# The down layer of a hybrid transformer step on one core: Strassen's products on pairs of token tiles

## The chip, the core and the metric

The kernel runs on one core of a Trainium2 chip. A core has TensorE (PE, 128 x 128 matmuls into PSUM), VectorE (DVE), ScalarE (ACT), GpSimd (POOL) and SyncE (SP, which issues most DMAs); all work from their own queues, in order, and wait for each other by semaphores. The metric is the device time of one execution in microseconds (us). The kernel before was timed three times: 1558.73, 1561.91 and 1562.32, median 1561.91.

## The reference

One inference step of one layer: a mixer (retention and sparse attention), then a feed-forward block. Only the second matmul of that block is changed:

```python
h = x + rms_norm(mix, g_post_mix)
f = rms_norm(h, g_pre_ffn) @ w_up
f = jnp.square(jax.nn.relu(f)) @ w_down
y = h + rms_norm(f, g_post_ffn)
```

There are 1024 prompt tokens and 128 new ones, so 9 tiles of 128 tokens; `w_up` is 1024 x 4096 and `w_down` 4096 x 1024, all in float32. `f` has 4096 features.

## The kernel before

Each float32 operand x of a matmul is split in two: hi = x rounded to the engine's format (a copy by ACT) and lo = x - hi (a subtraction by DVE or POOL). A product then takes three matmuls, hi x hi, hi x lo and lo x hi (`three_products`, L389 to L391).

The up layer goes in 16 steps of 256 features. It already uses Strassen's algorithm on its own blocks: per step seven products over the 8 prompt tiles (12 matmuls of 512 columns each) and the ninth tile directly ("odd"). Four blocks of the step's features (2 x 128 features by 2 x 512 tokens) are formed from PSUM banks and kept copies, passed through relu and square, and collected in `f_out`. The three blocks c11, c12 and c22 are formed by an addition and squared by DVE (`squared`, L2538), the fourth by ACT (`corner`). ACT issues the store of a step to the scratch `f_d` (L2428). POOL makes lo of the up layer's weights (L2145); DVE adds the up weights' combinations (L2128).

The down layer has the same 16 steps of 256 features. For step n SP loads 256 rows of `w_down` (`weights_in`, 1 MB) and the step's rows of f for all nine tiles (`rows_in`, 1.2 MB). ACT rounds the weights (`weights_hi`, L2760, 128 x 2048), POOL subtracts (L2804), ACT rounds the rows of three tiles at a time (`rows_hi`, L2769, 128 x 768), DVE subtracts (`rows_lo`, L2774). For each tile PE makes two column halves of 512, each of 2 feature blocks x 3 matmuls, into one of four double PSUM banks `dn`; DVE adds the 128 x 1024 result to the accumulator `acc` in SBUF (L2832; L2830 copies in the first step). PE waits for `added` of the tile four before. The order of every engine is written by hand: the functions `scalar`, `gpsimd`, `vector`, `tensor` of `up_programs` are followed by those of `down_programs`. Two functions, `room.down_hi` and `room.down_lo`, prepare the first weights and rows inside the last step of the up layer.

In the last step ACT sums the squares of each finished tile (L2789), POOL makes the reciprocal root (L2808, L2811), DVE multiplies by it and the gain (L2838), and DVE or POOL adds the residual h (L2816, L2844), which SP has loaded; SP stores the tile.

Of the kernel before, what the change touches and what calls it, by code (L numbers as in the profile page):

```python
# [23 lines left out]
P = 128  # L24
D = 1024
# [109 lines left out]
def hybrid_layer_kernel(nc, a, o):  # L135
# [18 lines left out]
    f_d = nc.dram_tensor("f_scratch", [STEPS, P, FC, TOK], F32, kind="Internal").ap()  # L154
# [1858 lines left out]
FIRST = [0, 1, 6, 7]  # L2013
FIRST_PRODUCTS = 9
# [22 lines left out]
class Room:  # L2037
# [361 lines left out]

def up_programs(nc, wide, paired, w_up, sem, ident, room, f_d):  # L2400
# [37 lines left out]
    def room_free(eng, n):  # L2438
# [492 lines left out]
```

## Time and profile before

| what | value |
|---|---|
| median of 3 runs | 1561.91 us (1558.73 to 1562.32) |
| profiled execution | 1557.19 us |
| its span | 1555.3 us |
| mean granted clock of TensorE | 0.987 |
| PE busy | 1495.5 us, 96% |
| DVE, ACT, POOL busy | 857.7, 708.1, 575.2 us |

The span runs from the first to the last instruction of the profiled execution; the time holds 1.9 us around it. A busy PE is one with a matmul in flight: matmuls overlap, each is shown 0.39 us long where the next starts 0.23 later. The granted clock is a share of 2.4 GHz; 0.50 is 1.2 GHz.

### The profile page before, as it was taken

Reading aid. Unit: us, or ns where it says so; the run is one execution under the profiler, and the core shown is the slowest. Engines: PE = TensorE matmul, PEld = TensorE weight load, DVE = VectorE, ACT = ScalarE, POOL = GpSimd, SP = SyncE. Lnnn points to the kernel's source line nnn. Section 1 sums busy time; section 2 is a strip of 40 time slices with the busy share of each in tenths; the row PEclk is TensorE's granted clock in tenths of the full one; section 3 lists DMA queues with packets and bytes.
Section 4 is the critical chain, followed back from the end, with each engine's and each line's share of the span. In section 5 each row is a group of like instructions: output and inputs, shape, how many; then the busy total and the mean of one; then the engine's idle time right before and its main releaser. Section 6 shows DMA issues by size and latency. Waiting matters only on the chain.

```text
span 1555.3 us, 22691 instructions
## 1 busy us (share of the span) xinstructions
PE 1495.5 (96%) x7956; PEld 1251.0 (80%) x7956; DVE 857.7 (55%) x1673; ACT 708.1 (46%) x1515; POOL 575.2 (37%) x509
## 2 busy tenths in 40 slices
PE   7998999999998999999999999999999999999994
PEld 6985787877777788978878888888888888888883
DVE  5278677777875555323574333342355555555557
ACT  5467577767676876624353333433322211121112
POOL 2311366656532541023455545554522122121215
PEclk9999999999998999999999999999999999999997
DMA  7310312121136542043312332233252231312216
GB/s 223 92 28 13 106 38 53 49 53 45 41 76 133 140 111 61 8 154 115 117 49 108 115 112 71 106 115 113 103 191 75 98 115 59 115 61 112 105 65 202
DMA packets 115304, 145.68 MB, mean 94 GB/s; under 512 B 46040, under 2 KB 93560, under 8 KB 110968
## 3 DMA queue, kind: packets, MB, share of 16 engines
q1 hardware_dynamic: 111120, 124.36, 25.7%
q10 hardware_dynamic: 4072, 19.88, 3.2%
q8 instruction: 64, 1.05, 0.3%
q14 instruction: 48, 0.39, 0.1%
HBM read 105.96 MB, written 38.25 MB: 93 GB/s over the span
## 4 chain that ended last, share of the span: by engine, by line
PE 63%; DVE 2%; ACT 2%; issue 2%; POOL 2%; SPq 1%; DMA 0%; POOLq 0%; ACTq 0%; DVEq 0%
PE wide L389 10%; PE wide L390 10%; PE wide L391 10%; PE paired L389 8%; PE paired L390 8%; PE paired L391 8%; PE paired L1984 4%; PE wide L1957 2%; PE paired L1968 2%; POOL acc L2816 0%; POOL ob_h L2322 0%; PE paired L2248 0%; DVE qT L1837 0%; SPq L1625 0%; DVE ob_mT_lo L2336 0%
## 5 line engine op out<-in xcount | busy, mean ns | idle before, releaser
L2804 POOL TENSOR_TENSOR aT_lo<-raw_u,aT_hi 128x2048 fp32r<-128x2048 f32 x16 | 73.8, 4613 | 294.7 <-ACT aT_hi L2760 294.7
L2769 ACT ACTIVATE xb_hi<-f_raw 128x768 fp32r<-128x768 f32 x48 | 40.7, 848 | 300.6 <-PE wide L391 153.7
L2145 POOL TENSOR_TENSOR wu_lo<-raw_u,wu_hi 128x512 fp32r<-128x512 f32 x64 | 86.5, 1371 | 164.5 <-ACT wu_hi L2140 164.5
L389 PE MATMUL paired<-w_hi,aT_hi 128*128 128x512 f32 x320 | 132.6, 414 | 1.4 <-PEq L424 1.4
L391 PE MATMUL paired<-w_hi,aT_lo 128*128 128x512 f32 x320 | 127.1, 397 | 0.0
L2832 DVE TENSOR_TENSOR acc<-wide,acc 128x1024 f32<-128x1024 f32 x68 | 83.3, 1224 | 79.0 <-PE wide L391 79.0
L390 PE MATMUL paired<-w_lo,aT_hi 128*128 128x512 f32 x320 | 126.6, 396 | 0.0
L2832 DVE TENSOR_TENSOR acc<-paired,acc 128x1024 f32<-128x1024 f32 x67 | 82.0, 1224 | 76.6 <-PE paired L391 76.6
L389 PE MATMUL wide<-aT_hi,xb_hi 128*128 128x512 f32 x288 | 112.2, 389 | 0.2 <-DVE acc L2832 0.2
L389 PE MATMUL paired<-aT_hi,xb_hi 128*128 128x512 f32 x288 | 112.1, 389 | 0.0
L391 PE MATMUL wide<-aT_hi,xb_lo 128*128 128x512 f32 x288 | 112.0, 389 | 0.0
L390 PE MATMUL paired<-aT_lo,xb_hi 128*128 128x512 f32 x288 | 112.0, 389 | 0.0
L390 PE MATMUL wide<-aT_lo,xb_hi 128*128 128x512 f32 x288 | 112.0, 389 | 0.0
L391 PE MATMUL paired<-aT_hi,xb_lo 128*128 128x512 f32 x288 | 112.0, 389 | 0.0
L1070 ACT ACTIVATE spare<-scores,sl_key 128x768 bf16<-128x768 f32 (+2 forms) x96 | 100.3, 1045 | 11.2 <-DVE sl_key L1176 3.8
L374 POOL TENSOR_TENSOR w_lo<-stage,w_hi 128x512 fp32r<-128x512 f32 (+1 forms) x50 | 64.4, 1304 | 100.1 <-ACT w_hi L369 100.1
L2145 POOL TENSOR_TENSOR wu_lo<-w_sum,wu_hi 128x512 fp32r<-128x512 f32 x60 | 90.1, 1532 | 0.0
L1199 DVE TENSOR_SCALAR_CACHE_REDUCE spare<-scores,sl_key 128x384 bf16<-128x384 f32 (+3 forms) x128 | 86.9, 679 | 4.6
L2564 DVE TENSOR_TENSOR f_out<-wide,stage 128x512 f32<-128x512 f32 x15 | 10.4, 691 | 126.6 <-PE wide L391 126.6
L389 PEld LDWEIGHTS paired<-w_hi,aT_hi 128*128 128x128 f32 x320 | 60.6, 189 | 18.2 <-issue 5.0
L1984 PE MATMUL paired<-vt,pT 128*128 128x64 f32 x576 | 72.9, 272 | 1.0 <-ACT pT L1741 0.6
L1984 PEld LDWEIGHTS paired<-vt,pT 128*128 128x128 f32 x576 | 70.0, 193 | 2.5 <-ACT pT L1741 1.2
(332 smaller groups left out, 4126.6 us busy)
## 6 DMA issues: line engine op xcount, KB each, us to landing
f_scratch<-f_out ACTq DMA_DIRECT2D x16, 1152.0 KB, 4.2
f_raw<-f_scratch SPq DMA_DIRECT2D x16, 1152.0 KB, 5.1
raw_u<-in_w_up SPq DMA_DIRECT2D x16, 1024.0 KB, 5.3
raw_u<-in_w_down SPq DMA_DIRECT2D x16, 1024.0 KB, 7.3
stage<-in_w_in SPq DMA_DIRECT2D x32, 256.0 KB, 3.3
stage<-mix_scratch SPq DMA_DIRECT2D x9, 512.0 KB, 4.1
h_scratch<-ob_h SPq DMA_DIRECT2D x9, 512.0 KB, 2.9
out<-acc SPq DMA_DIRECT2D x9, 512.0 KB, 5.0
```

The costliest lines, as they stand in the source:

```text
L374: self.nc.gpsimd.tensor_tensor(lo, raw, hi.bitcast(F32), ALU.subtract).then_inc(self.lo_done, 1)
L389: nc.tensor.matmul(out, lhs[0], rhs[0], start=first, stop=False, skip_group_check=onto)
L390: nc.tensor.matmul(out, lhs[0], rhs[1], start=False, stop=False, skip_group_check=onto)
L391: return nc.tensor.matmul(out, lhs[1], rhs[0], start=False, stop=last, skip_group_check=onto)
L1070: nc.scalar.activation(act_junk[:, 0:P * (t + 1)], score[t][:], ACT.Sign, scale=-1.0, bias=limit, accum_out=c_sum[:, n:n + 1]).then_inc(sl ...
L1199: nc.vector.tensor_scalar(dve_junk[:, 0:cells.shape[1]], cells, limit, None, ALU.is_ge, ALU.add, accum_out=c_sum[:, n:n + 1]).then_inc(sl_ ...
L1957: mm = nc.tensor.matmul(qk[u % 2][:, c0:c0 + w], qT[:, (t + 1) % 2, KV * m + g], kT[k][:, g, c0:c0 + w], start=(k == 0), stop=(k == 1))
L1984: mm = nc.tensor.matmul(po[:, h * HD:(h + 1) * HD], pT[:, n % 3, k * P:(k + 1) * P], vt[:, k0 + k, 64 * g:64 * g + 64], start=(k0 + k == 0 ...
L2145: self.nc.gpsimd.tensor_tensor(self.room.wu[1][:, s], self.source(i), self.room.wu[0][:, s].bitcast(F32), ALU.subtract).then_inc(self.lo_d ...
L2769: nc.scalar.activation(fT[0][:, q % 2], raw_f[n % 2][:, :, g * GT:(g + 1) * GT], ACT.Copy).then_inc(f_hi, 1)
L2804: nc.gpsimd.tensor_tensor(wd[1][n % 2], raw_d, wd[0][n % 2].bitcast(F32), ALU.subtract).then_inc(d_lo, 1)
L2832: nc.vector.tensor_tensor(acc[:, t], dn[d % 4][:], acc[:, t], ALU.add).then_inc(added, 1)
```

## The change

Two steps of 256 features are taken together as a double step d. In it the matrix of f^T has blocks by step (n = 0, 1: which half of the contraction inside a product) and by feature block (first or second 128 of a step), and the weights are B11, B12 (first feature blocks, left and right 512 columns), B21, B22 (second). Token tile k is paired with tile k+4. For such a pair Strassen's (Winograd's) form needs seven products in place of eight:

- of the rows: A11, S1, S3, A12, S2, S4, A22, where the S are sums and differences of the four blocks. They don't depend on the weights, so the up layer forms them, and stores seven blocks per pair of tiles (`COMB = 7`), 3968 columns a step where it stored 2304. DVE does it with three `add`s of 128 x 512 after c22 (`sums`), one later (`last_sum`), and one of 128 x 128 for the odd tile (`odd_sum`).
- of the weights: B11, T1, B21, T3, T2, B22, T4. DVE makes the four T per double step (`weight_sum`, 128 x 1024); ACT and POOL split all seven (128 x 1024 each).
- each product is 2 (steps) x 3 matmuls of 512 columns into one PSUM bank. Three of them go on a bank that holds an earlier product (T2 on the bank of B11, B22 on that of T1, T4 on that of T3); so each waits until DVE has added that earlier product.
- DVE adds every one of the seven banks to one of the accumulators c11, c12, c21, c22 or to a common part `acc_u`, which is added to the other three quarters once, in the last double step (`spread`).
- the ninth tile (the odd one) is computed with four products of the plain weights and of B22 with T3.

The rows come per tile pair (`rows_hi`/`rows_lo` of 128 x 1792), and the store of a step is issued after the third kept copy of the next step, not after the odd tile's.

```diff
+COMB = 7
+A11C, S1C, S3C, A12C, S2C, S4C, A22C = range(COMB)
+PAIR = COMB * P
+ODD = 4 * PAIR
+ROW = ODD + 3 * P
...
+        def sums(n):
+            if n == 0:
+                dve.wait_ge(f_act, 1)
+            dve.wait_ge(marked, mark["c22", n])
+            add(block(n, S1C), a21, block(n, A22C), ALU.add)
+            add(block(n, S3C), a21, block(n, A11C), ALU.subtract)
+            dve.wait_ge(marked, mark["S1", n])
+            add(block(n, S2C), block(n, S1C), block(n, A11C), ALU.subtract)
...
     def store(act, n):
-        act.wait_ge(squared_done, 3 * (n + 1))
+        act.wait_ge(marked, max(mark["S4", n], mark["odd", n]))
...
+SPLIT_ORDER = ("B11", "B21", "T1", "T3", "T2", "B22", "T4")
+PRODUCTS = (("B11", A11C, "a"), ("T1", S1C, "b"), ("B21", A12C, "c"), ("T3", S3C, "d"), ("T2", S2C, "a"), ("B22", S4C, "b"),
+            ("T4", A22C, "d"))
...
+    units = [(d, k) for d in range(LAST_STEP) for k in (0, 1, ODD_TILE, 2, 3)] + [(LAST_STEP, k) for k in (0, 1, 2, 3, ODD_TILE)]
...
+    def weights_in(sp, d):
+        for n in (1, 0):
+            if d >= 1:
+                sp.wait_ge(d_lo, COMB * d)
...
+            sp.dma_start(raw_d[:, n], down_rows(w_down, (2 * d + n) * FB)).then_inc(d_in, 16)
...
+        weights_hi(act, 0, "B22")
+        weights_hi(act, 0, "T4")
+        for u, (d, k) in enumerate(units):
+            if u + 1 < len(units):
+                rows_hi(act, u + 1)
+            if d < LAST_STEP:
+                for w in {1: ("B11", "B21"), ODD_TILE: ("T1", "T3"), 3: ("T2", "B22", "T4")}.get(k, ()):
+                    weights_hi(act, d + 1, w)
+            elif k != ODD_TILE:
+                sums(2 * k)
+                sums(2 * k + 1)
...
+        weight_sum(dve, 0, "T4")
+        for u, (d, k) in enumerate(units):
+            if u + 1 < len(units):
+                rows_lo(dve, u + 1)
+            if d == LAST_STEP and 1 <= k < ODD_TILE:
+                normalize(2 * k - 2)
+                normalize(2 * k - 1)
+            if k != ODD_TILE:
+                add_pair(u, d, k)
+                if d == LAST_STEP:
+                    spread(u, k)
+            else:
+                add_odd(u, d, 0)
+                add_odd(u, d, 1)
+            if d < LAST_STEP:
+                for w in {1: ("T1", "T3"), ODD_TILE: ("T2",), 2: ("T4",)}.get(k, ()):
+                    weight_sum(dve, d + 1, w)
...
+                if name in opened:
+                    pe.wait_ge(added, sums_before[u] + {"a": 1, "b": 2, "d": 4}[name])
```

**ACT at the turn from up to down.** Before (xb_hi<-f_raw are rows, aT_hi<-raw_u weights of down, L2467 to L2516 belong to up's last step):

```order
L2760 ACTIVATE aT_hi<-raw_u_2239 128x2048 [waits ml_product,ix_relued]
L2769 ACTIVATE xb_hi_2234<-f_raw0_2254 128x768 [waits ml_product,ix_iw_out]
L2467 ACTIVATE stage<-wide0 128x256 [waits ix_p_turned,ml_product]
L2469 ACTIVATE stage<-stage 128x256 [waits ix_p_kept_lo]
L2460 ACTIVATE f_out1_2253<-paired1 128x512 [waits ix_added,ml_product]
L2462 ACTIVATE f_out1_2253<-f_out1_2253 128x512 [waits ix_s_scored]
L2516 ACTIVATE f_out1_2253<-wide0 128x2x128 [waits ix_p_turned]
L2428 DMA f_scratch<-f_out1_2253 128x2304 [waits ix_past_in1,ix_p_new,ix_s_weighted]
L2769 ACTIVATE xb_hi_2234<-f_raw0_2254 128x768 [waits ml_product,ix_iw_out]
```

And now (raw_d are plain weights, t_sum the T, w_all the rows of a pair):

```order
L2889 ACTIVATE xb_hi_2234<-t_sum0_2260 128x1024 [waits ml_product,ml_u_sum]
L2504 ACTIVATE stage<-wide0 128x256 [waits ix_p_turned,ml_product]
L2506 ACTIVATE stage<-stage 128x256 [waits ix_p_kept_lo]
L2889 ACTIVATE xb_hi_2234<-t_sum1_2261 128x1024 [waits ml_product,ml_u_sum]
L2889 ACTIVATE aT_hi<-t_sum2_2262 128x1024 [waits ml_product,ml_u_sum]
L2497 ACTIVATE f_out1_2253<-paired1 128x4x128 [waits ix_added,ml_product]
L2499 ACTIVATE f_out1_2253<-f_out1_2253 128x4x128 [waits ix_s_scored]
L2559 ACTIVATE f_out1_2253<-wide0 128x256 [waits ix_p_turned]
L2465 DMA f_scratch<-f_out1_2253 128x3968 [waits ix_past_in1,ix_p_new,ix_s_weighted]
L2889 ACTIVATE aT_hi<-raw_d_2257 128x1024 [waits ml_product,ix_relued]
L2889 ACTIVATE aT_hi<-t_sum0_2260 128x1024 [waits ml_product,ml_u_sum]
L2907 ACTIVATE wu_hi_2241<-w_all_2258 128x1792 [waits ml_product,ix_q_kept]
```

The rows of pair 1 (last line) now stand behind the store of the last step and two weights.

**DVE in a steady double step.** Before, one lo of 768 (xb_lo) and three adds alternate:

```order
L2774 TENSOR_TENSOR xb_lo_2235<-f_raw0_2254,xb_hi_2234 128x768 [waits ix_q_turned]
L2832 TENSOR_TENSOR acc_2257<-paired0,acc_2257 128x1024 [waits ix_q_hi]
L2832 TENSOR_TENSOR acc_2257<-wide1,acc_2257 128x1024 [waits ix_q_hi]
L2832 TENSOR_TENSOR acc_2257<-wide0,acc_2257 128x1024 [waits ix_q_hi]
L2774 TENSOR_TENSOR xb_lo_2235<-f_raw0_2254,xb_hi_2234 128x768 [waits ix_q_turned]
```

Now, from the last add of pair 1 (L3008) to the first of pair 2:

```order
L3008 TENSOR_TENSOR acc5_2268<-wide0,acc5_2268 128x512 [waits ix_z_kept_lo,ix_q_hi]
L2927 TENSOR_TENSOR t_sum0_2260<-raw_d_2257 128x1024 [waits ix_wT_in,ix_relued]
L2927 TENSOR_TENSOR t_sum1_2261<-raw_d_2257 128x1024 [waits ix_wT_in,ix_relued]
L2913 TENSOR_TENSOR aT_lo<-w_all_2258,aT_hi 128x1792 [waits ix_q_turned]
L3008 TENSOR_TENSOR stage<-wide1,stage 128x512 [waits ix_z_kept_lo,ix_q_hi]
L3008 TENSOR_TENSOR stage<-paired0,stage 128x512 [waits ix_z_kept_lo,ix_q_hi]
L2927 TENSOR_TENSOR t_sum2_2262<-raw_d_2257,t_sum0_2260 128x1024 [waits ml_u_sum,ix_wT_in,ix_relued]
L2913 TENSOR_TENSOR wu_lo_2242<-w_all_2258,wu_hi_2241 128x1792 [waits ix_q_turned]
L3008 TENSOR_TENSOR acc2_2265<-paired0,acc2_2265 128x512 [waits ix_z_kept_lo,ix_q_hi]
```

Three weight sums and two lo of 1792 stand where one lo of 768 stood; the lo of pair 3 (L2913, second) comes ahead of pair 2's first add.

**ACT in the last double step.** Before, the squares (L2789) follow each other, with one piece of rows between:

```order
L2769 ACTIVATE xb_hi<-f_raw_2255 128x768 [waits ix_q_hi,ix_q_kept] x2
L2789 ACTIVATE dump,fn_st<-acc 128x1024 [waits ix_z_kept_lo]
L2789 ACTIVATE dump,fn_st<-acc 128x1024 [waits n_lo,ix_z_kept_lo] x2
L2769 ACTIVATE xb_hi<-f_raw_2255 128x768 [waits ix_q_hi,ix_q_kept]
L2789 ACTIVATE dump,fn_st<-acc 128x1024 [waits n_lo,ix_z_kept_lo] x6
```

Now the squares (L2955) of two tiles stand ahead of the rows (L2907) of each following pair:

```order
L2907 ACTIVATE wu_hi<-w_all 128x1792 [waits ix_q_hi,ix_q_kept]
L2955 ACTIVATE fn_dump,fn_st<-acc_2263 128x1024 [waits ix_z_kept_lo]
L2955 ACTIVATE fn_dump,fn_st<-acc_2267 128x1024 [waits n_lo,ix_z_kept_lo]
L2907 ACTIVATE aT_hi<-w_all 128x1792 [waits ix_q_hi,ix_iw_out]
L2955 ACTIVATE fn_dump,fn_st<-acc_2264 128x1024 [waits n_lo,ix_z_kept_lo]
L2955 ACTIVATE fn_dump,fn_st<-acc_2268 128x1024 [waits n_lo,ix_z_kept_lo]
L2907 ACTIVATE wu_hi<-w_all 128x1792 [waits ix_q_hi,ix_q_kept]
```

The first L2907 is pair 1's rows, the second pair 2's; before pair 2's rows ACT waits for pair 0's finished tiles.

## Rows read from the trace of the kernel before

**Rows 1.** The page, first part: busy time, share of the span, instructions.

```profile
PE 1495.5 (96%) x7956; PEld 1251.0 (80%) x7956; DVE 857.7 (55%) x1673; ACT 708.1 (46%) x1515; POOL 575.2 (37%) x509
```

**Rows 2.** Windows: stretch, length, busy of each engine (count), clock, DMA share, GB/s.

```profile
1200.00:1500.00 300.00, 300.00 (x1325) 248.43 (x1324) 167.38 (x148) 53.09 (x49) 55.35 (x12) 1.00 0.26 96
```

**Rows 3.** Groups by line and shape, 1200 to 1500: busy, mean ns, idle before.

```profile
L389 PE MATMUL wide<-aT_hi,xb_hi 128*128 128x512 f32 x224 | 87.1, 389 | 0.0
...
L2832 DVE TENSOR_TENSOR acc<-wide,acc 128x1024 f32<-128x1024 f32 x56 | 68.6, 1225 | 67.3 <-PE wide L391 67.3
...
L2804 POOL TENSOR_TENSOR aT_lo<-raw_u,aT_hi 128x2048 fp32r<-128x2048 f32 x12 | 55.4, 4613 | 238.4 <-ACT aT_hi L2760 238.4
...
L2774 DVE TENSOR_TENSOR xb_lo<-f_raw,xb_hi 128x768 fp32r<-128x768 f32 x37 | 35.1, 950 | 0.0
L2769 ACT ACTIVATE xb_hi<-f_raw 128x768 fp32r<-128x768 f32 x37 | 31.4, 849 | 247.0 <-PE paired L391 126.3 <-PE wide L391 120.8
L2760 ACT ACTIVATE aT_hi<-raw_u 128x2048 fp32r<-128x2048 f32 x12 | 22.8, 1903 | 0.0
```

**Rows 4.** Timeline of the turn from up to down: start, duration, [idle before].

```profile
1133.95 4.61 POOL L2804 TENSOR_TENSOR aT_lo<-raw_u,aT_hi 128x2048 fp32r<-128x2048 f32 x1 [9.22 <-ACT aT_hi L2760]
...
1134.19 0.69 DVE L2571 TENSOR_TENSOR f_out<-paired,stage 128x512 f32<-128x512 f32 x1 [6.99 <-PE paired L391]
...
1134.91 4.20 DVE L2538 SCALAR_TENSOR_TENSOR f_out<-f_out 128x512 f32<-128x512 f32 x1
...
1139.76 0.19 PEld L389 LDWEIGHTS paired<-aT_hi,wu_hi 128*128 128x128 f32 x1 [0.23 <-DVE f_out L2576]
...
1142.78 0.48 PE L389 MATMUL paired<-aT_hi,xb_hi 128*128 128x512 f32 x1
```

**Rows 5.** Timelines of DVE and of POOL in up; POOL's L2145, min/median/max ns.

```profile
843.66 0.69 DVE L2128 TENSOR_TENSOR w_sum<-w_sum,raw_u 128x512 f32<-128x512 f32 x1
...
846.00 1.77 DVE L2128 TENSOR_TENSOR w_sum<-raw_u 128x512 f32<-128x512 f32 x1
...
845.49 1.74 POOL L2145 TENSOR_TENSOR wu_lo<-raw_u,wu_hi 128x512 fp32r<-128x512 f32 x1
...
L2145 POOL TENSOR_TENSOR wu_lo<-w_sum,wu_hi x60: 1282/1730/1753, 802.4 to 1118.0; 128x512 fp32r<-128x512 f32 x60
```

**Rows 6.** DMA issues from 1177 to 1186: packets, KB each, us to landing.

```profile
DMA packets 416, 2.23 MB, mean 248 GB/s; under 512 B 32, under 2 KB 32, under 8 KB 288
...
raw_u<-in_w_down SPq DMA_DIRECT2D x1, 1024.0 KB, 7.1
```

**Rows 7.** Windows at two granted clocks, and PE's timeline at two gaps.

```profile
490.30:500.60 10.30, 9.49 (x42) 8.27 (x42) 6.17 (x23) 5.60 (x21) 0.00 (x0) 0.50 0.32 64
...
792.40:800.00 7.60, 5.32 (x28) 4.49 (x28) 5.28 (x5) 6.93 (x11) 1.74 (x3) 1.00 0.61 192
...
1538.30:1555.00 16.70, 0.00 (x0) 0.00 (x0) 13.89 (x12) 3.46 (x6) 6.49 (x7) 0.50 0.86 288
...
490.95 0.48 PE L1957 MATMUL wide<-kT_hi,qT 128*128 128x128 f32 x1 [1.91 <-DVE kT_lo L1837]
...
794.78 1.09 PE L2248 MATMUL paired<-ident,ob_x 128*128 128x128 f32 x8 [2.28 <-DVE ob_x L2351]
```

**Rows 8.** Timeline of the end, by engine.

```profile
1529.49 0.19 PEld L389 LDWEIGHTS wide<-aT_hi,xb_hi 128*128 128x128 f32 x1 [0.64 <-DVE acc L2832]
...
1534.85 0.39 PE L391 MATMUL paired<-aT_hi,xb_lo 128*128 128x512 f32 x1
...
1529.47 1.06 ACT L2789 ACTIVATE dump<-acc 128x1024 f32<-128x1024 f32 x1 [7.89 <-DVE acc L2832]
1530.44 0.18 ACT L2789 ACTIVATION_READ_ACCUMULATOR dump<-acc 128x1 f32 x1
...
1550.98 1.28 DVE L2854 SCALAR_TENSOR_TENSOR acc<-acc,fn_st,raw_u 128x1024 f32<-128x1024 f32 x1
...
1530.53 2.42 POOL L2816 TENSOR_TENSOR acc<-acc,raw_u 128x1024 f32<-128x1024 f32 x1
```

More of the change, by code:

```diff
@@ L2523, in scalar @@
         keep_odd(STEPS - 1)
+        store(act, STEPS - 1)
     def gpsimd(pool):
@@ new lines, in gpsimd, with add, add_pair, spread @@
+        for k in range(3):
+            rescale(2 * k)
+            rescale(2 * k + 1)
+            residual(2 * k)
+            residual(2 * k + 1)
+        for i in range(6, TILES):
+            rescale(i)
+        residual(6)
+    def vector(dve):
+        def add(cells, bank, u, i, opens):
+            dve.wait_ge(dn_done, products[u] + i + 1)
+            if opens:
+                nc.vector.tensor_copy(cells, bank).then_inc(added, 1)
+            else:
+                dve.wait_ge(added, sums_before[u] + max(0, i - 1) if i < 4 else sums_before[u])
+                nc.vector.tensor_tensor(cells, bank, cells, ALU.add).then_inc(added, 1)
+        def add_pair(u, d, k):
+            b, zero = banks[k % 2], d == 0
+            if zero and k in (1, 2):
+                dve.wait_ge(f_stored[k - 1], 16 * (STEPS // 2))
+            c11, c12, c21, c22 = acc[k][:, left], acc[k][:, right], acc[k + 4][:, left], acc[k + 4][:, right]
+            add(c11, b["a"], u, 0, zero)
+            add(c22, b["b"], u, 1, zero)
+            add(c11, b["c"], u, 2, False)
+            add(c22, b["d"], u, 3, False)
+            add(acc_u[k], b["a"], u, 4, zero)
+            add(c12, b["b"], u, 5, zero)
+            add(c21, b["d"], u, 6, zero)
+        def spread(u, k):
+            for i, cells in enumerate((acc[k][:, right], acc[k + 4][:, left], acc[k + 4][:, right])):
+                dve.wait_ge(added, sums_before[u] + COMB)
+                nc.vector.tensor_tensor(cells, cells, acc_u[k], ALU.add).then_inc(added, 1)
+        def add_odd(u, d, m):
+            add(acc[PT][:, (left, right)[m]], banks[0]["dc"[m]], u, m, d == 0)
+        def normalize(i):
+            t = finals[i]
+            if i == 0:
@@ L2857, in vector @@
-        for q in range(Q - 1):
-            rows_lo(dve, q + 1)
-            if q == Q - 2:
-                for t in range(3):
-                    normalize(t)
-            for j in range(3):
-                add(3 * q + j)
-        last = 3 * (Q - 1)
-        normalize(3)
-        residual(3)
-        normalize(4)
-        add(last)
-        residual(4)
-        normalize(5)
-        add(last + 1)
-        residual(5)
-        weigh(6)
-        add(last + 2)
-        scaled_residual(6)
-        weigh(7)
```

494 lines of the change are left out of this document (312 added, 182 removed).

## The prediction

> **What bounds the kernel now.** I read the page's busy shares first, then the stages by windows, then the groups of the down layer, then order of time at its two ends. TensorE (PE) is busy for 96% of the span [rows 1], and 300 us inside the down layer hold 1325 matmuls with no gap at the full granted clock [rows 2]: one matmul of 512 columns every 300/1325 = 0.2265 us. There VectorE (DVE) is busy 167 us of 300, ScalarE (ACT) 53, GpSimd (POOL) 55, and DVE's adds wait for PE, not the reverse [rows 2, 3]. So a matmul removed from this layer is worth its 0.2265 us as long as PE is never kept waiting by the three others, which hold the operands' second halves (ACT rounds to "hi", DVE or POOL subtracts to get "lo"). The layer starts at 1142.78 [rows 4], its last matmul starts at 1534.85, and the span ends 20.1 us after that matmul's end, at 1555.3 [rows 8]. The profiled execution took 1557.19, 4.7 below the median of the runs shown (1561.91).
>
> **Part 1, matmuls.** Before: 9 tiles x 2 column halves x 2 features x 3 = 108 per step, 216 per pair of steps. After: 4 tile pairs x 7 products x 6, plus 24 for the odd tile = 192. Eight double steps: 192 fewer, x 0.2265 = **-43.5 us**, if nothing stalls. A product is 6 matmuls, 1.36 us; a tile pair 9.51; the odd tile 5.44.
>
> **Part 2, what the others must deliver.** Durations of new shapes by line through neighbours of the same kind. DVE with 512, 768 and 1024 elements: 0.69, 0.95, 1.22 [rows 3, 5], so 1.04 per 1000; an lo of 1792 is 2.0 (bounds 0.95 and 2.2, the same slope at 2048), a weight sum of 1024 is 1.2. ACT: 0.85 for 768, 1.90 for 2048 [rows 3], so 1.68 for 1792, 1.06 for 1024. POOL: 1.28 for 512, 4.61 for 2048 [rows 3, 5], so 2.4 for 1024. Two consecutive operations of one engine overlap by 0.1. A product's result reaches another engine 0.2 after PE turned to the next (a matmul shows 0.39 for 0.2265 of spacing). In a double step of 43.5 us this makes some 34 us on DVE, 15 on ACT and 17 on POOL. All fit; only collisions can cost.
>
> The collision: a DVE operation with both inputs in SBUF waits while POOL runs. POOL ran 1133.95 to 1138.56, and DVE's squaring, begun at 1134.91, took 4.20 instead of 0.69 [rows 4]. When both queue, they alternate: POOL's at 845.49 takes 1.74 after DVE's, DVE's at 846.00 takes 1.77, not 0.69 [rows 5]; of 60 POOL splits the median is 1.73 against 1.28 at least [rows 5]. DVE's adds from PSUM stay at 1.22 [rows 3]. The Trainium skill, "SBUF — State Buffer", Who interferes with whom, says the same: a VectorE instruction with two SBUF inputs and a GpSimd one that reads SBUF exclude each other for a whole instruction. By that rule, the trace agrees, the change pays with DVE's time for what it adds to POOL: seven splits of 1024 in a double step (16.8 us) instead of two of 2048 (9.2). The order of the changed kernel puts DVE's next-but-one lo *ahead* of the adds of the current pair, and product 5 of each pair (T2, on the bank of product 1) waits for the first add. So the pair stalls when first add ends later than 5.44 us after its start.
>
> **Part 3, steady double steps.** Time t from the start of pair 0. POOL splits T2 (-1.4 to 1.0), B22 (to 3.4) and T4; ACT, after T4's hi, rounds the rows of pair 1 until 2.9; DVE's lo gets in at 3.4, ends 5.3, first add 5.9: PE stalls 0.5. T4's lo ends at 7.5 and releases 2 MB of weights. Before, 2.2 MB in two issues landed 7.1 us after the second [rows 6]; so they are there at 14.3, and B11 and B21 are split by 20.3, just before DVE is done with pair 1 (20.4). DVE: sums T1, T3, lo of pair 2 until 24.7; PE needs it at 25.0: no stall. Then POOL's T1 lo (to 26.9), DVE's sum T2 (to 28.0), POOL's T3 lo (waiting longer, to 30.3), DVE's lo of pair 3 (to 32.2), first add of pair 2 to 32.9; product 5 was due at 30.45: **stall 2.4**. Pair 3 has no stall. Sum over seven double steps with a successor, or predecessor: 7 x 2.4 + 7 x 0.5 = **+20.2** (bounds: 7 x 0.2 = 1.4 without exclusion; 7 x 5, twice 2.4 and more, if the weights land 3 us later).
>
> **Part 4, the turn from up to down**, in the trace's own times. Step 15 of up: c12 is added at 1134.19. DVE's squaring waits for POOL's B11 (to 1136.1), then POOL's B21 goes first (1136.7 to 1139.0), DVE: lo of pair 0 to 1140.9, sum T1 to 1142.0, and only then c22, which up's last product waits for: it starts at 1142.65 instead of 1139.76 [rows 4]. POOL T1 to 1145.6, DVE sum T3 and T2 to 1147.8, S1C, then alternately POOL T3, S3C, POOL T2, S2C, S4C, the odd sum at 1155.2. ACT stands at the store of step 15 until then, and behind the store are B22, T4 and the rows of pair 1 (0.5+1.06+1.0+1.7: 1159.3). POOL's T4 holds DVE until 1161.4, lo of pair 1 to 1163.3, first add 1164.0. PE did four products of pair 0 from 1145.5 and waits from 1152 to 1164.1 for the fifth, due at 1142.78+5.44 = 1148.2: **+15.9** (bounds: 4.2, the same chain with no exclusion; 20, if each lo meets one more POOL operation).
>
> **Part 5, the last double step.** ACT's queue is rows(k+1), squares of two tiles, rows(k+2); the squares wait for the last add and a spread add of pair k. From the end E of a pair: add to E+0.9, spread to 1.6, squares of two tiles (1.06+0.18 each [rows 8]; the second waits for the third spread) to 4.15, rows hi to 5.85, lo to 7.9, two normalizations of 1.28 (as the last line of DVE's kind in [rows 8]) to 10.3, first add to 10.9. Product 5 is due at E+5.44: **5.5** twice; before the odd tile the rows are 768 wide, **3.6**. Sum +14.6 (bounds 11, 18). The 0.6 stall in the last step of before [rows 8] goes. After the last matmul come one add, ACT's square, and DVE normalize, normalize, weigh, residual, scaled residual with POOL's 2.42 [rows 8] in between: 9.2, and 3.0 for the store as before (1550.98+1.28 to 1555.3): 12.2 against 20.1, **-7.9**.
>
> **Other edits.** Up's steps: DVE gets four sums of 0.69, alternating with POOL, up to 1122; its next due work is at 1125.9. The store leaves 2 us later with 2.0 instead of 1.2 MB and is due 16 us after. Nothing: PE waits nowhere there today, and DVE has those gaps. If the cover fails, c22 late by 1 us costs 15.
>
> **Part 6, the clock.** PE was granted 1.2 GHz from 490.3 for 10.3 us around a gap of 1.91 us, though it worked densely again; a gap of 2.28 at 792.5 left it at 2.4 [rows 7]. After PE's end it fell, too [rows 7]. The 12 us wait of part 4 will lower it, and each us at 1.2 GHz after resuming costs half of it: between 0 and 5, I take 3. The three waits of part 5: four products at half speed cost up to 4.1 a pair, I take 2 each: +6 (0 to 17, the odd tile included). Waits of 2.4: 0 (up to 1.7 each). The skill, "TensorE: Matmul & The Clock Gate", Why this matters for your kernels, asks that gaps between bursts stay short, else the array falls back; by it, parts 4 and 5 pay and part 3 does not.
>
> **Sum.** -43.5 +20.2 +15.9 +14.6 -0.6 -7.9 = -1.3 at the full clock, +9 for the clock: +7.7, 1557.19 -> 1564.9 for a profiled execution, and with the same 4.7 between it and the median: **1569**.
>
> **Rivals.** (A) The waits overlap as summed, but the clock stays at 2.4 GHz: 1561.9-1.3 = 1560.6. For: 2.28 us without a fall. Against: 12 us is far more. (B) The exclusion hardly bites, because the orders fall otherwise: bounds of parts 3 and 4, 18.8+11.7 less: 1569-30-3 = 1536. For: DVE has 9 us free per double step; against: rows 5. (C) Half: the 2.4 of part 3 vanish, for its order hangs on 0.1 us here and there: 1552. (D) Slower than all: PE falls to 1.2 GHz in the stalls of pair 2 and in most of the last double step: 7 x 1.7 + 11 + 2 more: 1594. It decides as soon as waits of 2.4 lower the clock.
>
> **How the numbers follow.** Forecast 45%, A 19%, C 14%, B 10%, D 12%. 0.3% is 4.7 us, about what a measurement tells. Faster: B, C and a little of A, 0.27; same: most of A and the forecast's lower edge, 0.19; slower: the rest, 0.54. Cases of both signs count, so the forecast's own range is 1560 to 1580; the range for all is 1543 to 1590.
>
> **What would show it.** Right: matmuls 192 fewer; a PE gap near 12 us between T3 and T2 of the first pair, released by DVE's first add; gaps of 2 to 3 before product 5 of each pair 2 (bank of paired0, right half), of 0.5 in pair 0; 5.5, 5.5, 3.6 in the last double step; DVE's 1792-wide lo at 2.0 alone and 4 beside POOL; granted clock at 0.5 after the first gap. Wrong: no gaps in the steady double steps (B, C), lo durations all at 2.0, or PE waiting for weights (then the landing of 2 MB was mis-sized), or waits inside the up layer.

## The result and the profile after

Before 1560.74 us median (4 runs, 1558.73 to 1562.32), after **1582.62 us** (4 runs, 1581.24 to 1585.71): ratio 1.0144, 95% interval 1.0123 to 1.0164. The kernel is 22 us (1.4%) slower; 7.7 had been forecast. The direction, the range for all cases (1543 to 1590) and most of the terms held; the size did not, and the median lies above the forecast's own range (1560 to 1580). The profiled execution took 1582.76 with a span of 1581.0, so it took 25.6 longer than that of before (1557.19).

The page's first part after [rows 1], of span 1581.0 us, busy time, share and instructions:

```profile
PE 1475.8 (93%) x7764; PEld 1224.8 (77%) x7764; DVE 1018.4 (64%) x1881; ACT 752.9 (48%) x1547; POOL 678.9 (43%) x553
```

PE has less to do, and DVE 160 us more than before. The same 300 us stretch of the down layer as in [rows 2] (stretch, length, busy of PE, PEld, DVE, ACT, POOL with counts, clock, DMA share, GB/s), and its groups of POOL and DVE [rows 3] (mean ns behind the comma):

```profile
1200.00:1500.00 300.00, 279.38 (x1184) 225.25 (x1183) 229.16 (x241) 88.91 (x73) 127.13 (x42) 0.98 0.36 125
```

```profile
L3008 DVE TENSOR_TENSOR acc<-wide,acc 128x512 f32<-128x512 f32 x95 | 65.1, 685 | 42.6 <-PE wide L391 42.6
L2975 POOL TENSOR_TENSOR aT_lo<-t_sum,aT_hi 128x1024 fp32r<-128x1024 f32 x18 | 62.0, 3449 | 103.0 <-ACT aT_hi L2889 103.0
L2913 DVE TENSOR_TENSOR wu_lo<-w_all,wu_hi 128x1792 fp32r<-128x1792 f32 x12 | 39.4, 3284 | 12.6 <-ACT wu_hi L2907 12.6
...
L2913 DVE TENSOR_TENSOR aT_lo<-w_all,aT_hi 128x1792 fp32r<-128x1792 f32 x13 | 26.2, 2018 | 0.0
...
L2975 POOL TENSOR_TENSOR aT_lo<-raw_d,aT_hi 128x1024 fp32r<-128x1024 f32 x9 | 21.7, 2413 | 26.1 <-ACT aT_hi L2889 26.1
```

POOL's split of 1024 columns takes 2.41 us where it meets nobody (the plain weights, raw_d) and 3.45 on the mean for the T (t_sum), which come while DVE makes sums and lo. DVE's lo of 1792 takes 2.02 into one buffer (rows of pairs 0 and 2) and 3.28 on the mean into the other (pairs 1 and 3): that one stands beside POOL. The adds from PSUM, with one SBUF input, stay at 0.685.

**Where PE waits.** The waits of PE in the down layer and at its start, by what ended them (total, times, longest):

```profile
PE paired L389 <- DVE acc L3008: 31.0, 16, 5.1
PE paired L389 <- DVE acc L3005: 13.7, 2, 11.5
PE paired L389 <- DVE aT_lo L2913: 3.6, 3, 1.4
PE paired L389 <- DVE f_out L2642: 2.3, 1, 2.3
PE wide L389 <- POOL xb_lo L2975: 0.7, 1, 0.7
```

All but 0.7 us ends with DVE. A bracket of the profile shows only the idle time after a matmul that is drawn 0.39 us long, though the next could start 0.2265 after its start. So in what follows a wait is the bracket plus 0.16, where no bracket is quoted. The turn from up to down [rows 4], in order of time (start, duration, [idle before]), first DVE, then ACT, then PE:

```profile
1135.88 0.69 DVE L2635 TENSOR_TENSOR a<-paired,stage 128x512 f32<-128x512 f32 x1 [4.25 <-PE paired L391]
...
1137.70 4.21 DVE L2913 TENSOR_TENSOR aT_lo<-w_all,aT_hi 128x1792 fp32r<-128x1792 f32 x1
1141.83 1.21 DVE L2927 TENSOR_TENSOR t_sum<-raw_d 128x1024 f32<-128x1024 f32 x1
1142.97 0.68 DVE L2642 TENSOR_TENSOR f_out<-paired,stage 128x512 f32<-128x512 f32 x1
...
1148.77 3.48 DVE L2583 TENSOR_TENSOR f_out<-a,f_out 128x512 f32<-128x512 f32 x2
1152.17 3.85 DVE L2583 TENSOR_TENSOR f_out<-f_out 128x512 f32<-128x512 f32 x3
...
1160.10 4.05 DVE L2913 TENSOR_TENSOR wu_lo<-w_all,wu_hi 128x1792 fp32r<-128x1792 f32 x1 [2.95 <-ACT wu_hi L2907]
1164.08 0.68 DVE L3005 COPY acc<-paired 128x512 f32<-128x512 f32 x1
...
1156.05 0.33 ACTq L2465 DMA_DIRECT2D f_scratch<-f_out  x1
...
1143.70 0.50 PE L389 MATMUL paired<-aT_hi,wu_hi 128*128 128x512 f32 x1 [2.27 <-DVE f_out L2642]
...
1164.90 0.77 PE L389 MATMUL paired<-aT_hi 128*128 128x512 f32 x1 [11.49 <-DVE acc L3005]
```

Every time here is 1.7 later than on the axis of before: c12 is added at 1135.88, there at 1134.19 [rows 4]. Less that, up's last product starts at 1142.0 (1142.65 had been put), the store is issued at 1154.4 (from 1155.2 on), and the first add ends at 1163.1 (1164.0). The chain is the forecast one, up to 0.9 us shorter. A steady double step, product 5 of pair 2, DVE, POOL and PE:

```profile
1234.27 7.49 POOL L2975 TENSOR_TENSOR xb_lo<-t_sum,xb_hi 128x1024 fp32r<-128x1024 f32 x2 [2.26 <-ACT xb_hi L2889]
...
1237.29 2.22 DVE L2927 TENSOR_TENSOR t_sum<-raw_d,t_sum 128x1024 f32<-128x1024 f32 x1
1239.43 4.21 DVE L2913 TENSOR_TENSOR wu_lo<-w_all,wu_hi 128x1792 fp32r<-128x1792 f32 x1
1243.57 0.68 DVE L3008 TENSOR_TENSOR acc<-paired,acc 128x512 f32<-128x512 f32 x1
...
1244.30 0.50 PE L389 MATMUL paired<-aT_hi 128*128 128x512 f32 x1 [2.34 <-DVE acc L3008]
```

DVE's sum (1.2 us alone) waits for one POOL split, its lo for the next, and the add on which PE waits stands behind both.

**Where the clock falls.** Windows of after, of the turn, of pair 2 in double steps 0 to 6 and of the last double step (PE's busy time is the third number, the granted clock the third from the end):

```profile
1156.80:1170.50 13.70, 5.60 (x13) 4.51 (x14) 7.59 (x8) 4.76 (x5) 4.66 (x2) 0.50 0.89 356
1194.40:1197.80 3.40, 3.34 (x8) 2.66 (x9) 2.17 (x5) 0.00 (x0) 0.00 (x0) 0.50 0.82 259
1245.60:1249.00 3.40, 3.40 (x10) 2.63 (x9) 1.37 (x3) 0.00 (x0) 0.00 (x0) 0.50 0.58 233
1293.40:1296.80 3.40, 3.40 (x10) 2.65 (x9) 1.98 (x4) 0.00 (x0) 0.00 (x0) 0.50 0.80 265
1342.90:1346.30 3.40, 3.36 (x15) 2.75 (x16) 2.71 (x5) 0.00 (x0) 0.00 (x0) 1.00 0.83 255
1390.10:1393.50 3.40, 3.40 (x15) 2.82 (x16) 2.73 (x5) 0.00 (x0) 0.00 (x0) 1.00 0.83 261
1440.20:1443.60 3.40, 3.40 (x9) 2.65 (x8) 1.49 (x3) 0.00 (x0) 0.00 (x0) 0.51 0.57 230
1487.90:1491.30 3.40, 3.40 (x10) 2.65 (x9) 1.98 (x4) 0.00 (x0) 0.00 (x0) 0.51 0.78 262
1522.10:1528.90 6.80, 5.08 (x12) 4.01 (x13) 4.15 (x6) 0.00 (x0) 5.62 (x2) 0.50 0.36 92
1539.10:1545.90 6.80, 4.78 (x11) 3.79 (x12) 4.45 (x7) 0.00 (x0) 5.68 (x2) 0.50 0.31 69
1556.20:1559.60 3.40, 3.19 (x8) 2.51 (x9) 2.17 (x5) 0.00 (x0) 3.40 (x2) 0.50 0.16 40
```

Behind five of the seven nearly equal waits (2.35 to 2.52 us) PE works at 1.2 GHz (8 to 10 matmuls in 3.4 us), behind two at 2.4 (15). PE's busy time at the low clock is 5.60 (turn) + 16.94 (the five) + 13.05 (last double step) = 35.6 us, of which half is lost: 17.8, where 9 had been put. Timed from the end of one wait at product 5 to the end of the next, double steps with equal waits take 48.65 and 48.72 us behind a spell (from 1244.30 and from 1438.73) and 47.15 without one (from 1342.94): so a spell costs 1.5 to 1.6 directly, a little less than the 1.7 of the halving.

All four runs of after have a mean granted clock of 0.972 to 0.974, the 23 runs of before taken beside the experiments 0.984 to 0.988, so the spells aren't a chance of the profiled execution.

### The profile page after: what moved, and what is told of

Its sections match the earlier page's. It is cut to its first block, busy times and chain, and to the rows that moved or that the text cites. A ratio compares the mean times of both kernels' runs of the same rounds, so it can differ in the third digit from the quotient of the medians.

```text
span 1581.0 us, 22978 instructions
## 1 busy us (share of the span) xinstructions
PE 1475.8 (93%) x7764; PEld 1224.8 (77%) x7764; DVE 1018.4 (64%) x1881; ACT 752.9 (48%) x1547; POOL 678.9 (43%) x553
## 4 chain that ended last, share of the span: by engine, by line
PE 54%; DVE 8%; issue 6%; ACT 3%; SPq 1%; POOL 1%; DMA 0%; DVEq 0%; ACTq 0%; POOLq 0%
PE wide L389 9%; PE wide L390 9%; PE wide L391 9%; PE paired L389 6%; PE paired L391 6%; PE paired L390 6%; PE paired L1984 4%; DVE wu_lo L2913 2%; PE wide L1957 2%; PE paired L1968 2%; ACT wu_hi L2907 1%; DVE aT_lo L2913 1%; DVE t_sum L2927 1%; DVE acc L3008 1%; DVE stage L3008 0%
## 5 line engine op out<-in xcount | busy, mean ns | idle before, releaser
L2975 POOL TENSOR_TENSOR aT_lo<-t_sum,aT_hi 128x1024 fp32r<-128x1024 f32 x24 | 81.2, 3389 | 127.6 <-ACT aT_hi L2889 127.6
L3008 DVE TENSOR_TENSOR acc<-wide,acc 128x512 f32<-128x512 f32 x116 | 79.5, 685 | 52.2 <-PE wide L391 52.2
L389 PE MATMUL paired<-aT_hi,wu_hi 128*128 128x512 f32 x232 | 93.4, 402 | 10.6 <-DVE acc L3008 8.3
L391 PE MATMUL paired<-aT_hi,wu_lo 128*128 128x512 f32 x232 | 91.5, 394 | 0.0
L390 PE MATMUL paired<-aT_lo,wu_hi 128*128 128x512 f32 x232 | 91.4, 394 | 0.0
L389 PE MATMUL wide<-aT_hi,wu_hi 128*128 128x512 f32 x192 | 76.2, 397 | 0.0
L390 PE MATMUL wide<-aT_lo,wu_hi 128*128 128x512 f32 x192 | 75.8, 395 | 0.0
L391 PE MATMUL wide<-aT_hi,wu_lo 128*128 128x512 f32 x192 | 75.5, 393 | 0.0
L1867 POOL TENSOR_TENSOR near<-bias,scores 128x2048 f32<-128x2048 f32 (+1 forms) x8 | 34.4, 4301 | 88.7 <-DVE mn L1809 68.9
L391 PEld LDWEIGHTS paired<-w_hi,aT_lo 128*128 128x128 f32 x320 | 60.1, 188 | 14.0
L2907 ACT ACTIVATE aT_hi<-w_all 128x1792 fp32r<-128x1792 f32 x16 | 27.2, 1697 | 91.3 <-PE wide L391 91.3
```

Source lines behind the costliest of these rows:

```text
L389: nc.tensor.matmul(out, lhs[0], rhs[0], start=first, stop=False, skip_group_check=onto)
L390: nc.tensor.matmul(out, lhs[0], rhs[1], start=False, stop=False, skip_group_check=onto)
L391: return nc.tensor.matmul(out, lhs[1], rhs[0], start=False, stop=last, skip_group_check=onto)
L2907: nc.scalar.activation(fT[q % 2][0], raw_f[q % 2], ACT.Copy).then_inc(f_hi, 1)
L2975: nc.gpsimd.tensor_tensor(s[1], source[w] if w in source else t_sum[w][:], s[0].bitcast(F32), ALU.subtract).then_inc(d_lo, 1)
L3008: nc.vector.tensor_tensor(cells, bank, cells, ALU.add).then_inc(added, 1)
```

## The experiments

The diffs are shortened: constant switches that turn the other orders off are folded away. Each ratio goes by runs of before taken alongside (medians 1560.74 for after, 1558.43 for lo later, small POOL splits, last double step and turn, 1558.76 for the other three), so between kernels the ratios compare better than the medians. "From P8" is the time from the last product of the up layer that waits (the matmul at 1143.70 above; 1139.8 before, [rows 4]) to the span's end. It leaves out the part of the program ahead of the change, which in these profiles ends anywhere from 1138.8 to 1145.3, and with it the wait of 2.3 for c22. Spans and times from P8 are of one profile each.

| kernel | median us | ratio to before [95%] | span | from P8 |
|---|---|---|---|---|
| before | 1560.74 | | 1555.3 | 415.5 |
| after | 1582.62 | 1.0144 [1.0123, 1.0164] | 1581.0 | 437.3 |
| lo later | 1554.54 | 0.9971 [0.9958, 0.9985] | 1551.1 | 409.0 |
| small POOL splits | 1551.95 | 0.9958 [0.9942, 0.9974] | 1550.8 | 407.0 |
| last double step | 1568.41 | 1.0069 [1.0042, 1.0096] | 1567.4 | 426.0 |
| turn | 1578.97 | 1.0135 [1.0118, 1.0152] | 1576.9 | 438.1 |
| waits filled | 1576.53 | 1.0110 [1.0096, 1.0124] | 1575.2 | 429.9 |
| three orders | 1547.33 | 0.9922 [0.9910, 0.9935] | 1547.1 | 401.8 |
| rows first | 1541.09 | 0.9884 [0.9868, 0.9899] | 1539.2 | 395.3 |

### The lo of the next rows after two adds

```diff
         def add_pair(u, d, k, after={}):
             add(c11, b["a"], u, 0, zero)
             add(c22, b["b"], u, 1, zero)
+            after.get(1, lambda: None)()
...
+            late = 0 < u and d < LAST_STEP and k != ODD_TILE
+            if late:
+                after[1] = lambda: rows_lo(dve, u + 1)
-            if u + 1 < len(units):
+            elif u + 1 < len(units):
                 rows_lo(dve, u + 1)
```

> Steady double steps only: DVE's lo for the next pair stands behind the second add of the current pair instead of ahead of the first. Theory (waits come from DVE's order and its exclusion with POOL, and the clock falls because of the waits): the waits before product 5 of pair 2 (7 x 2.5 = 17.4) and of pair 0 (7 x 0.65 = 4.6) vanish, at most 0.4 appears before product 7; the 1.2 to 1.6 at the start of pair 2 in double steps 1, 3, 5 stays; the five spells of 1.2 GHz in the steady part (17 us, so 8.5 lost) go too: 1582.6 - 22 - 8.5 + 1 = 1553. Rival 1 (the lower clock belongs to the new stream of matmuls, not to waits): 1561. Rival 2 (product 5 waits for the bank as such, whatever DVE does first): no change, 1582.

Measured 1554.54, where the theory had it, and under the kernel before. The lo is no shorter (4.17 us beside POOL); it no longer stands ahead of the adds that free the banks. First DVE, then PE in that kernel's timeline:

```profile
1251.54 4.17 DVE L2913 TENSOR_TENSOR wu_lo<-w_all,wu_hi 128x1792 fp32r<-128x1792 f32 x1
...
1257.05 0.47 PE L389 MATMUL wide<-aT_hi 128*128 128x512 f32 x1 [0.72 <-DVE acc L3008]
```

And the clock stays up from 1200 to 1480:

```profile
1200.00:1480.00 280.00, 274.75 (x1197) 223.48 (x1196) 226.56 (x243) 92.00 (x76) 127.47 (x45) 1.00 0.40 137
```

PE's waits from P8 on are 21.5 us less than in after, and the five spells at 1.2 GHz are gone. One of 3.4 us has come behind c22's wait, where after has none. In all PE's work at the low clock from P8 on falls from 35.6 to 20.2 us, which is worth 7.7: 29.2 together, against 28.3 from P8. What part 3 had put at 20.2 is worth this much and more.

### POOL's splits made small

```diff
-                nc.gpsimd.tensor_tensor(s[1], source[w] if w in source else t_sum[w][:], s[0].bitcast(F32),
-                                        ALU.subtract).then_inc(d_lo, 1)
+                raw = source[w] if w in source else t_sum[w][:]
+                some = slice(0, 16 if d >= 2 else 512)
+                nc.gpsimd.tensor_tensor(s[1][:, :, some], raw[:, :, some], s[0][:, :, some].bitcast(F32),
+                                        ALU.subtract).then_inc(d_lo, 1)
```

> From double step 2 on POOL subtracts only 16 of every 512 columns of the seven weight matrices (the rest of the lo halves is left as it was), so POOL hardly runs; the order of every engine is unchanged. Theory (exclusion of DVE and POOL makes the steady waits): the waits of 2.5 in pair 2 of double steps 1 to 6, the 1.2 to 1.6 at its start in 1, 3, 5 and most of the 0.65 in pair 0 vanish (22), DVE's lo of 1792 takes 2.0 everywhere from there, and 7 of lower clock goes: 1554; only the turn, the first pair 2 and the last double step keep their waits. Rival (DVE's order and load alone make the waits): 1578 or more.

Measured 1551.95. This kernel leaves out most of the weights' lo halves from double step 2 on; it serves to time the others, not to be used. From 1200 to 1500 the lo of pairs 1 and 3 takes what that of pairs 0 and 2 always took:

```profile
L2913 DVE TENSOR_TENSOR aT_lo<-w_all,aT_hi 128x1792 fp32r<-128x1792 f32 x14 | 28.3, 2023 | 2.9 <-ACT aT_hi L2907 2.9
L2913 DVE TENSOR_TENSOR wu_lo<-w_all,wu_hi 128x1792 fp32r<-128x1792 f32 x13 | 26.7, 2053 | 14.6 <-ACT wu_hi L2907 14.6
```

Nothing of DVE's work or order was touched, so the waits of the steady double steps come from POOL's splits. POOL's end also releases the next weights' load, so this run alone doesn't part an earlier load from the exclusion; DVE's own durations above show the exclusion. That is the rule of the Trainium skill, "SBUF — State Buffer", Who interferes with whom; the runs agree with it.

### Squares and normalizations one pair later

```diff
-            elif k != ODD_TILE:
-                sums(2 * k)
-                sums(2 * k + 1)
+            elif k > 0:
+                sums(2 * k - 2 if k != ODD_TILE else 6)
+                sums(2 * k - 1 if k != ODD_TILE else 7)
...
+            if d == LAST_STEP and 1 <= k < ODD_TILE:
+                after[3] = lambda: normalize(2 * k - 2)
+                after[4] = lambda: normalize(2 * k - 1)
```

(and the lo of the next rows after two adds, in this double step alone.)

> Last double step only: ACT rounds the rows of pair k+2 ahead of the squares of pair k; DVE's lo stands behind the second add and the two normalizations behind the fourth and fifth. Theory: the waits of 5.3, 5.3 and 3.4 shrink to about 2 in all, the 1.2 GHz spells there (13 us with PE at work, 6.5 lost) mostly go, DVE ends 1 to 2 us later after the last matmul: 1582.6 - 12 - 5 + 1.5 = 1567. Rival 1 (the clock stays low there all the same): 1572. Rival 2 (DVE itself has 11 us of work per 9.5 us pair, so only the place of the wait moves): 1578 or more.

Measured 1568.41, close to the theory's 1567, in part by luck: 6.8 us of waits are left where 2 had been put, and before was 2.3 us faster in this set of runs than in after's. In the last double step PE waits 0.9, 2.2, 0.9 and 2.8 instead of 5.3, 5.3 and 3.4, and over it the clock is whole:

```profile
1505.00:1545.00 40.00, 33.88 (x146) 26.75 (x145) 38.97 (x41) 10.93 (x15) 19.10 (x17) 1.00 0.56 181
```

That is 7.2 of waits and 6.5 of clock. The end gives 2.9 back: from the start of the last matmul to the span's end 16.6 us instead of 13.7, since DVE, behind with what was put off, comes to the last matmul's add 2.5 us late. Net 10.8; from P8 11.3.

### Squarings and store of up's last step after the first adds of down

```diff
             if n == STEPS - 1:
                 room.down_sums(dve)
-            sums(n)
+            else:
+                sums(n)
...
-        last_sum(STEPS - 1)
-        odd_sum(STEPS - 1)
+        room.up_late = (lambda: sums(late)), (lambda: last_sum(late)), (lambda: odd_sum(late))
...
+            if u == 0:
+                after[3], after[4], after[5] = room.up_late
```

(on ACT, the store behind the roundings of double step 0 and of pair 1.)

> The turn from up to down only: ACT issues the store of step 15 after the rows of pair 1, DVE makes the five sums of step 15 between the adds of pair 0, and its lo of pair 1 behind the second add. Theory (the 11.7 us wait is the chain sums, store, B22, T4, rows, lo, add): product 5 is then due by T2's split and waits for 2 to 4 us, the wait of 2.3 for c22 stays; 8.5 of wait and 2.8 of lower clock less: 1571. Rival (POOL's seven splits or the landing of the weights bound the turn): 1580 or more, with PE waiting for POOL's lo.

Measured 1578.97: a miss. The interval of its ratio overlaps that of after, so no gain is shown, and the rival had named both, POOL's splits and the landing of the weights. The 11.7 us wait shrank to 0.9, 0.8 and 2.6 (all three now released by POOL's lo), but a new one stands in front of pair 2. DVE, then PE in that kernel:

```profile
1174.30 2.36 DVE L2928 TENSOR_TENSOR t_sum<-raw_d 128x1024 f32<-128x1024 f32 x2 [4.61 <-DMA raw_d<-in_w_down]
1177.92 2.84 DVE L2914 TENSOR_TENSOR aT_lo<-w_all,aT_hi 128x1792 fp32r<-128x1792 f32 x1 [1.26 <-ACT aT_hi L2908]
...
1180.81 0.79 PE L389 MATMUL paired<-xb_hi,aT_hi 128*128 128x512 f32 x1 [6.41 <-DVE aT_lo L2914]
```

The weights of double step 1 were issued at 1158.2 and landed after 14.4 us on the median of their two halves (5.9 in the kernel after), together with the 2 MB store and the rows; DVE and ACT stood at them, with the rows of pair 2 queued behind. The clock fell behind the waits of 2.6 and 6.6, the second time for 10 us:

```profile
1156.20:1159.60 3.40, 3.40 (x8) 2.72 (x9) 3.40 (x7) 0.00 (x0) 0.00 (x0) 0.50 0.33 81
1176.70:1186.90 10.20, 6.09 (x14) 4.79 (x15) 8.98 (x5) 4.67 (x4) 10.20 (x4) 0.50 0.29 94
```

The waits are 4.3 less. At the low clock PE worked 10.5 us more (46.2), 5.3 lost; but little of that lies at the turn, where its work in these two spells is 9.5 against 8.9 in after (1156.8 and 1194.4 above). Another 3.4 stands behind c22's wait, unchanged at 2.3, and 6.5 in the steady double steps, where nothing was changed: there the clock fell behind six of six waits of 2.5, in after behind four of the same six. From P8 it is 0.8 longer than after. So whether such a wait lowers the clock differs between profiles with the same waits.

### The wait filled with a product

```diff
+                if w == "T3" and k == 2 and d < LAST_STEP:
+                    chain(banks[k % 2][name], fT[k % 2], j, slot(d, w), True, True, False)
                 chain(banks[k % 2][name], fT[k % 2], j, slot(d, w), name not in opened, True,
                       name in opened).then_inc(dn_done, 1)
```

> In double steps 0 to 6 TensorE does the product T3 x S3 of pair 2 twice, opening the bank again each time, so the result is unchanged: 42 matmuls (7 x 1.36 = 9.5 us of TensorE work) more, put just before the product that waits for VectorE. The wait ends at the same time as before, since VectorE decides it, so the gap of 2.5 us shrinks to 1.1. Theory (the waits of 2.5 themselves lowered the clock in five of seven double steps, 1.7 us each): no spell at 0.50 in the steady double steps, nothing else moves, 1582.6 - 8.5 = 1574, although 42 matmuls were added. Rival (the spells are a budget of work or heat and come whatever the gaps are): five spells stay, 1582.6 +-1.5. Rival 2 (the extra product is not hidden): 1592.

Measured 1576.53, **some 5 us less with 42 matmuls more**: 0.34% by the ratios, whose intervals barely part, 6.1 by the medians. DVE decides the end of the wait as before; the bracket shows 0.96 where it showed 2.34, and PE goes on at 2.4 GHz. PE's timeline at the same place, and three of the seven windows, which all show 1.00:

```profile
1243.58 0.50 PE L389 MATMUL paired<-aT_hi 128*128 128x512 f32 x1 [0.96 <-DVE acc L3008]
```

```profile
1241.00:1247.00 6.00, 5.04 (x23) 3.85 (x22) 5.33 (x7) 0.00 (x0) 0.04 (x1) 1.00 0.49 156
1288.00:1294.00 6.00, 5.04 (x23) 3.86 (x22) 5.33 (x7) 0.00 (x0) 0.13 (x1) 1.00 0.46 143
...
1433.00:1439.00 6.00, 5.01 (x22) 3.82 (x21) 4.94 (x7) 0.00 (x0) 0.00 (x0) 1.00 0.47 153
```

From P8 it is 7.4 shorter. PE's work at the low clock there falls from 35.6 to 19.6 (8.0 gained), the wait of the turn and the small one ahead of it shrank by 1.4, and the waits in front of pair 2 grew by 1.9. So the spells in the steady double steps came from the waits, and neither of the two rivals stands.

### The three orders together

The three edits above in one kernel.

> The three orders together: next rows' lo after the first two adds in every double step, last double step with squares and normalizations one pair later, turn with the squarings and the last store of up later. The spans of the three alone were 29.9, 13.6 and 4.1 us shorter than that of the changed kernel (1581.0), and they touch different places except double step 0. Theory (they add): span 1533, median 1536 to 1541, 1.3% under the kernel before. The 6.6 us wait at 1174 of the turn kernel (rows of pair 2 behind the weight sums of double step 1, whose weights land 14 us after their issue) should be there again. Rival (one hides another: the wait saved comes back at the next product): 1550, no better than the first order alone.

Measured 1547.33, 0.8% under before, but some 9 us over the middle of the expectation. From P8 the three alone give -28.3 - 11.3 + 0.8 = -38.8; measured -35.5. They add, but for 3.3, of which 2.8 is the wait in front of pair 2 (a bracket of 9.20, in the turn's kernel 6.41). The expectation had added spans, in which the part ahead of the change differs by up to 6.5. The wait in front of pair 2 is back as foretold, larger:

```profile
1188.47 0.80 PE L389 MATMUL paired<-xb_hi,aT_hi 128*128 128x512 f32 x1 [9.20 <-DVE aT_lo L2914]
```

### Rows of pair 2 ahead of the next weights, in double step 0

```diff
-                for w in {1: ("T1", "T3"), ODD_TILE: ("T2",), 2: ("T4",)}.get(k, ()):
+                early = {1: ("T1", "T3"), ODD_TILE: ("T2",)} if d else {ODD_TILE: ("T1", "T3", "T2")}
+                for w in {**early, 2: ("T4",)}.get(k, ()):
```

(and the same on ACT.)

> The kernel with the three orders, and in double step 0 alone ScalarE rounds and VectorE subtracts the rows of pair 2 before they turn to the weights and weight sums of double step 1 instead of after. Theory (the turn kernel's wait of 6.6 us in front of pair 2 is two engines' queues standing at a load of weights that landed 14 us after its issue): that wait is under 1 us, and the spell at 0.50 behind it (10 us in the records) goes too, 6 + 3: 9 us less than the kernel with the three orders, about 1530. Rival (pair 2 waits for its own rows' load, which shares the queues with the weights and the last store): same time as the kernel with three orders, wait of 5 or more in the same place, now for rows from f_scratch.

Measured **1541.09**, 1.2% under before: the fastest of all. 6.2 less than the three orders, 6.5 from P8, where 9 had been expected. The wait in front of pair 2 is gone, but one of 3.50 stands at its fifth product, since the add that frees its bank is now behind three sums whose weights landed 13.1 and 16.7 us after their issue:

```profile
1180.55 2.36 DVE L2928 TENSOR_TENSOR t_sum<-raw_d 128x1024 f32<-128x1024 f32 x2 [1.89 <-DMA raw_d<-in_w_down]
...
1186.87 0.50 PE L389 MATMUL paired<-aT_hi 128*128 128x512 f32 x1 [3.50 <-DVE acc L3009]
```

The rival (pair 2 waits for its own rows) falls: its lo ran at 1173.14, seven us before the weights were there.

## Why the prediction was right or wrong

- **Part 1**: 192 matmuls fewer, as counted. The price is nearly right: from product 5 of pair 2 to the next one, two double steps without a spell took 47.15 and 48.64 us (from 1342.94 and 1390.09), less their waits of 3.2 and 4.7 44.0 and 43.9, where 192 x 0.2265 is 43.5. So each lasts 0.4 to 0.5 longer than summed, some 3 us in seven.
- **Part 2**, the exclusion: right, and shown by the small splits. Split alone 2.41 (2.4 had been taken), lo alone 2.02 (2.0) and 4.2 beside POOL (4).
- **Part 3**: at product 5 of pair 2, seven gaps of 2.35 to 2.52, 17.4 in all (7 x 2.4 = 16.8); in pair 0, 7 x 0.65 = 4.6 (3.5). Not foreseen: 1.2, 1.3 and 1.6 in front of pair 2 in double steps 1, 3 and 5 (the three on `aT_lo` above), 4.1: there DVE's sum waited for a split of freshly landed weights, and the lo of pair 2 behind it. "Lo later" and the small splits have none of the three.
- **Part 4**: 2.3 + 0.8 + 11.7 = 14.8 (15.9), by the steps as written, each up to 0.9 early.
- **Part 5**: 5.3, 5.3, 3.4 = 14.0 (14.6). After the last matmul's end 13.3 (12.2) against 20.1: -6.8 (-7.9).
- **Other edits**: "PE waits nowhere there" held for the store and the sums in up. A granted clock of 0.50 for 3.4 us at 795.0, behind a bracket of 2.27 that in before (2.28) left the clock at 2.4 GHz [rows 7], is worth 1.7 in this profile. It isn't the change's: the same wait stands in all nine profiles and is followed by such a spell in five of them (after, lo later, last double step, waits filled, rows first).
- **Part 6**, the clock: the step that failed. It took "Waits of 2.4: 0 (up to 1.7 each)", from the one wait of 2.28 in [rows 7] behind which the clock stayed. Five of seven paid nearly the whole 1.7 (1.5 to 1.6 timed directly): 8.5 us by the halving, where 0 had been put. The other two entries held: turn 5.6/2 = 2.8 (3), last double step 13.05/2 = 6.5 (6).

The sum by its own steps: -43.5 + 17.4 + 4.6 + 4.1 + 14.8 + 14.0 - 0.6 - 6.8 = +4.0 at the full clock (-1.3 had been put), and +17.8 for the clock (+9): +21.8. With the 1.7 at 795 that is 23.5 of the 25.6 between the two profiles. The 2.1 left fit the 3 us by which the double steps are longer than part 1 counts. Profile against profile the forecast is missed by 17.9 us (25.6 instead of 7.7): 8.8 is the clock, 5.3 the terms at the full clock (4.1 in front of pair 2, 1.1 behind the last matmul, the others nearly cancel), 1.7 the spell at 795, 2.1 the rest. Between the medians the miss is only 14, because the profiled execution of before lay 3.6 to 4.7 below its median and that of after at it; that is luck.

Rival D had named the point ("it decides as soon as waits of 2.4 lower the clock") and was given 12%. Its first half came true for five of seven waits, its second (most of the last double step at 1.2 GHz) did not; the truth lies midway between D and the forecast. The single row with a clock that stayed was read as a rule, though [rows 7] also held a wait of 1.91 around which it fell, and the same wait of 2.28, in the eight other profiles, lowered the clock in five. With two cases that contradict each other, the middle of the bounds (7 x 0.85 = 6) would have been the better entry. The forecast had likewise carried the 4.7 between the profile of before and its median over to the kernel after, whose profile lies at its median.

By the Trainium skill, "TensorE: Matmul & The Clock Gate", Why this matters for your kernels, which asks for short gaps between bursts, parts 4 and 5 pay and part 3 does not; the runs agree on 4 and 5 and contradict it on 3, in the turn's kernel too.

What stays open: why two of the seven nearly equal waits left the clock up; the rows shown don't set them apart. Open as well is where in a double step the 0.4 to 0.5 us go, and whether another order of the loads would end the last waits of double step 0; that wasn't tried.

## What to carry to other kernels

Fewer matmuls don't shorten a kernel bound by TensorE if the engine that frees its banks falls behind: put the adds that release a bank ahead of the work for the next tile, and count two-input VectorE work and GpSimd work from SBUF as one queue. Price each wait of TensorE at its length plus what the clock takes afterwards, and where one wait in the trace lowered it and another didn't, price it between both. When an order is moved to close one gap, look at which engine queue then stands at a late load, and compare stretches from a common instruction, not whole spans.

## What the runs showed of the hardware

- A wait of 2.3 to 2.5 us cost 60 to 70% more than its length: PE was granted 1.2 GHz for 3.4 us behind five of seven (1.5 to 1.7 lost each), in the turn's kernel behind six of six. It isn't a matter of length alone: in "last double step" waits of 2.2 and 2.8 left the clock up, and one and the same wait in the up layer (bracket 2.24 to 2.28) lowered it in five of nine profiles. Waits of 0.6 to 1.6 in the steady double steps never lowered it, in any of the kernels.
- Work put into a wait (42 matmuls) was not only free but gained some 5 us, by keeping the clock up.
- Two DVE operations in a row can each lose to POOL: a sum of 1024 took 2.22 instead of 1.22 and the lo behind it 4.21 instead of 2.02, as POOL went first both times (7.49 us for two splits of 2.4).
- Two loads of weights of 1 MB each landed 5.9 us after their issue on the median; issued beside a 2 MB store and three loads of rows they took 14.4 (turn) and 14.9 (rows first), the later of the two 16.7.
